# First attention of a two-block transformer kernel: its score products taken from high and low parts of queries and keys that are stacked over all 128 rows

## The reference, cut to what matters

```
def diff_attention_mixer(h, hc, w_in, lam, subln, w_out, lambda_init, ctx_out):
    ...
    q, k, v = project(h)
    qc, kc, vc = project(hc)
    q, k = apply_rope(q, cos, sin), apply_rope(k, cos, sin)
    ...
    def attend(qb, kb, vb):
        sc = jnp.einsum('blhid,bkhid->bihlk', qb, kb, preferred_element_type=jnp.float32) * scale
        p = jax.nn.softmax(sc, axis=-1)
        p = p[:, 0] - lam_full * p[:, 1]
        o = jnp.einsum('bhlk,bkhd->blhd', p.astype(vb.dtype), vb)
        o = rmsnorm(o, subln) * (1.0 - lambda_init)
        return o.reshape(o.shape[0], o.shape[1], DA_HEADS * DA_V_DIM)
```

## Time and profile before

| | |
|---|---|
| median of three runs | 2395.69 us (2393.03 to 2397.93) |
| profiled execution | 2393.02 us, its span 2391.1 us |
| TensorE busy | 2322.2 us, 97% of the span |
| granted TensorE clock, mean | 0.997 of full speed |
| VectorE, ScalarE, GpSimd busy | 1297.4, 971.0, 1340.2 us |
| the first attention's units | from 447.0 us (first score product) to about 650 us |

### The profile page before, as it was taken

One profiled execution on the slowest core, in us unless ns is written; L12 is line 12 of the kernel. 1 busy time (PEld: TensorE's weight loads), 2 busy tenths in 40 slices (PEclk: granted clock), 3 DMA queues, 4 the chain that ended last, 5 costly groups with the idle time before them and its releaser, 6 DMA issues.

```text
span 2391.1 us, 36091 instructions
## 1 busy us (share of the span) xinstructions
PE 2322.2 (97%) x14528; PEld 2068.9 (87%) x14528; DVE 1297.4 (54%) x2191; ACT 971.0 (41%) x1598; POOL 1340.2 (56%) x700
## 2 busy tenths in 40 slices
PE   7999999999989999999999998899999999999998
PEld 5888889777688888898888897799999999999998
DVE  8898296666578982966332035564324314534331
ACT  4322224455442332243223235454444444545443
POOL 3564465222135654654444442188879886468886
PEclk9999999999999999999999999999999999999999
DMA  6555362211025553625553331145555564345554
GB/s 271 211 192 178 110 219 85 71 62 54 27 80 212 194 176 110 220 93 187 192 178 108 98 93 62 45 168 185 176 166 179 180 195 150 98 148 187 182 178 135
DMA packets 97508, 350.09 MB, mean 146 GB/s; under 512 B 10944, under 2 KB 10944, under 8 KB 96960
## 3 DMA queue, kind: packets, MB, share of 16 engines
q1 hardware_dynamic: 97344, 347.81, 43.6%
HBM read 346.71 MB, written 1.05 MB: 145 GB/s over the span
## 4 chain that ended last, share of the span: by engine, by line
PE 62%; DVE 4%; ACT 2%; issue 1%; DMA 1%; POOL 1%; SPq 0%; DVEq 0%; ACTq 0%
PE psum L1573 20%; PE psum L1577 19%; PE psum L1574 19%; POOL w_lo L770 1%; PE psum L1922 1%; ACT w_hi L790 1%; PE psum L1894 1%; DMA w_raw<-in_ffn_out 0%; DVE psum L1131 0%; DVE psum L1211 0%; DVE h L1217 0%; PE psum L1902 0%; DVE u_lo L1431 0%; DVE pcomb L1404 0%; DVE stat L1489 0%
## 5 line engine op out<-in xcount | busy, mean ns | idle before, releaser
L770 POOL TENSOR_TENSOR w_lo<-w_raw,w_hi 128x1024 fp32r<-128x1024 f32 (+3 forms) x696 | 1340.0, 1946 | 1034.0 <-ACT w_hi L790 1033.2
L1573 PE MATMUL psum<-u_hi,w_hi 128*128 128x256 f32 (+2 forms) x2912 | 972.4, 334 | 10.9 <-POOL w_lo L770 7.7
L1577 PE MATMUL psum<-u_lo,w_hi 128*128 128x256 f32 (+2 forms) x2912 | 948.2, 326 | 3.5 <-DVE u_lo L1203 2.2
L1574 PE MATMUL psum<-u_hi,w_lo 128*128 128x256 f32 (+2 forms) x2912 | 946.5, 325 | 0.0
L790 ACT ACTIVATE w_hi<-w_raw 128x1024 fp32r<-128x1024 f32 (+1 forms) x522 | 537.4, 1032 | 438.8 <-PE psum L1577 343.2
L1573 PEld LDWEIGHTS psum<-u_hi,w_hi 128*128 128x128 f32 x2912 | 554.3, 190 | 78.8 <-issue 27.6
L1577 PEld LDWEIGHTS psum<-u_lo,w_hi 128*128 128x128 f32 x2912 | 553.6, 190 | 52.3 <-DVE u_lo L1203 5.3
L1574 PEld LDWEIGHTS psum<-u_hi,w_lo 128*128 128x128 f32 x2912 | 554.4, 190 | 45.5 <-issue 3.4
L1573 PE MATMUL psum<-gu_hi,w_hi 128*128 128x256 f32 (+1 forms) x1188 | 379.4, 319 | 0.2 <-POOL w_lo L770 0.2
L1574 PE MATMUL psum<-gu_hi,w_lo 128*128 128x256 f32 (+1 forms) x1188 | 378.1, 318 | 0.0
L1577 PE MATMUL psum<-gu_lo,w_hi 128*128 128x256 f32 (+1 forms) x1188 | 378.1, 318 | 0.0
(11 more groups left out here) (173 smaller groups left out, 1984.5 us busy)
## 6 DMA issues: line engine op xcount, KB each, us to landing
w_raw<-in_ffn_in SPq DMA_DIRECT2D x264, 512.0 KB, 3.5
w_raw<-in_ffn_out SPq DMA_DIRECT2D x96, 448.0 KB, 3.4
ada_hi<-in_ada_w SPq DMA_DIRECT2D x48, 512.0 KB, 5.2
ada_lo<-in_ada_w SPq DMA_DIRECT2D x48, 512.0 KB, 5.2
w_raw<-in_ffn_out SPq DMA_DIRECT2D x48, 512.0 KB, 3.6
ada_out<-in_ada_w SPq DMA_DIRECT2D x32, 512.0 KB, 3.8
w_raw<-in_b_qkv SPq DMA_DIRECT2D x30, 512.0 KB, 3.5
w_raw<-in_da_in SPq DMA_DIRECT2D x24, 512.0 KB, 3.5
```

The source lines that it names most:

```text
L770: last = pool.tensor_tensor(w_lo[:, slot, w], w_raw[:, slot, w], w_hi[:, slot, w].bitcast(F32), ALU.subtract)
L1573: mm(out, w_hi[:, slot, w], x_hi, start=start and n == 0, stop=False)
L1574: mm(out, w_lo[:, slot, w], x_hi, start=False, stop=False)
L1577: last = mm(out, w_hi[:, slot, w], x_lo, start=False, stop=stop and n == len(ks) - 1)
```

## The change

The scores of the first attention are made from high and low parts. For each head and each map m, `qa[:, room, m]` holds the high part of the map's query on its own 64 rows and the low part on the other 64. `ka[:, room, m]` holds the key's high part on both halves, `kb[:, room, m]` the key's low part on the map's own rows and zeros on the others. Two `float32r` products over 128 rows then give high by high plus low by high (L1994) and high by low (L1995). There are two rooms, for even and odd heads.

ScalarE makes the high copies, 64 x 512 each: two for a query, four for a key (a new list entry `split`). GpSimd makes the low parts, two subtractions of 64 x 512 for a query and two for a key, and once two memsets of `kb`. In the list the query's and key's `split` are put about one clock tick after their `rot`, and not before the scores of head s-2 are reached. On GpSimd a split comes after the low parts of all weight tiles up to the one behind the newest that the projections have begun (`behind`), and before all later tiles. TensorE waits for GpSimd (`split_part`) in place of the rotary result. The rotary temporaries, the raw q and k, v, probabilities and their like move to other places in SBUF; the raw key has one buffer, so ScalarE's evacuation of a key waits for GpSimd's split of the key before it.

```diff
@@ mixer_plan
+    def split(it):
+        nonlocal splits
+        splits += 1
+        it["split_n"], it["behind"] = splits, newest + 1
+        add("split", it)
+    def split_due():
+        while unsplit and unsplit[0][1] <= clock and scored >= 4 * unsplit[0][0]["s"] - 5:
+            split(unsplit.pop(0)[0])
...
+        if op == "rot" and kind == "da":
+            unsplit.append((it, clock + 1))
@@ GpSimd
+        def split_rest(x):
+            n = split_steps(x) - 2
+            pool.wait_ge(lo_ready, x["behind"] + 1)
+            pool.wait_ge(split_hi, x["split_n"])
+            if x["split_n"] == 1:
+                for m in range(2):
+                    pool.memset(kb[map_rows(1 - m), :, m, :].bitcast(F32), 0.0).then_inc(split_part, 1)
+                    pool.wait_ge(split_part, m + 1)
+            room, src = x["s"] % 2, item_stage(x)
+            for m in range(2):
+                own, across = map_rows(m), map_rows(1 - m)
+                if x["what"] == "q":
+                    pool.tensor_tensor(qa[across, room, m, :], src[own, :], qa[own, room, m, :].bitcast(F32),
+                                       ALU.subtract).then_inc(split_part, 1)
+                else:
+                    pool.tensor_tensor(kb[own, room, m, :], src[own, :], ka[own, room, m, :].bitcast(F32),
+                                       ALU.subtract).then_inc(split_part, 1)
+                pool.wait_ge(split_part, n + m + 1)
...
+        for x in (x for op, x, _ in plans["da"][0] if op == "split"):
+            rests(done, x["behind"] + 1)
+            done = x["behind"] + 1
+            split_rest(x)
+        rests(done, N_TILES)
@@ ScalarE
+                if kind == "da" and x["what"] != "v" and room_user(x):
+                    act.wait_ge(split_part, split_steps(room_user(x)))
...
+                elif op == "split":
+                    act.wait_ge(S["qk_ready"], x["rope_n"])
+                    if x["s"] >= 2:
+                        act.wait_ge(S["s_ready"], 4 * (x["s"] - 1))
+                    room, src = x["s"] % 2, item_stage(x)
+                    for m in range(2):
+                        own, across = map_rows(m), map_rows(1 - m)
+                        if x["what"] == "q":
+                            last = scalar.activation(qa[own, room, m, :], src[own, :], ACT.Copy)
+                        else:
+                            scalar.activation(ka[own, room, m, :], src[own, :], ACT.Copy)
+                            last = scalar.activation(ka[across, room, m, :], src[own, :], ACT.Copy)
+                    last.then_inc(split_hi, 1)
@@ TensorE
             def item_ready(it):
-                if it["rope"]:
+                if kind == "da":
+                    pe.wait_ge(split_part, split_steps(it))
+                elif it["rope"]:
                     pe.wait_ge(S["qk_ready"], it["rope_n"])
...
                     elif kind == "da":
+                        room, q0 = st["s"] % 2, x["qt"] * 128
                         for m in range(2):
-                            rows = slice(64 * m, 64 * m + 64)
-                            q0, k0 = place_of(st["q"][0]) + x["qt"] * 128, place_of(st["k"][0])
-                            last = mm(out[:, m, :], q_st[rows, q0:q0 + 128], k_st[rows, k0:k0 + n], start=True, stop=True)
+                            query = qa[:, room, m, q0:q0 + 128]
+                            mm(out[:, m, :], query, ka[:, room, m, 0:n], start=True, stop=False)
+                            last = mm(out[:, m, :], query, kb[:, room, m, 0:n], start=False, stop=True)
```

More of the change, by code:

```diff
@@ L258, in prepare_due @@
                 prepare(n)
-                return
+                break
+        split_due()
     def prepare_all(of):
@@ L265, in prepare_all @@
             if n is None:
+                while any(it is o for it, _ in unsplit for o in of):
+                    split(unsplit.pop(0)[0])
                 return
@@ L277, in mixer_plan @@
     add("first", first)
+    newest = max(it["t"] for it in first)
     clock += 16
@@ L638, in item_stage, with map_rows, room_user, split_steps @@
             off = it["g"] * SEQ
-            return vT[:, off:off + n]
+            return v_raw[it["kind"]][:, off:off + n]
+        if it["kind"] == "da":
+            return da_q[:, it["s"] % 2, :] if it["what"] == "q" else da_k[:, :]
         off = place_of(it)
         return (q_st if it["what"] == "q" else k_st)[:, off:off + n]
+    def map_rows(m):
+        return slice(64 * m, 64 * m + 64)
+    def room_user(it):
+        n = it["s"] - (2 if it["what"] == "q" else 1)
+        return next((x for op, x, _ in plans["da"][0] if op == "split" and x["what"] == it["what"] and x["s"] == n), None)
+    def split_steps(it):
+        return 2 * it["split_n"] + 2
     def latents(it):
+        if it["kind"] == "da":
+            return item_stage(it)[:, LAT]
         off = place_of(it) + width(it["tok"]) - SEQ
```

46 lines of the change are left out of this document (37 added, 9 removed).

## The result

The changed kernel takes 2408.22 us (median of 6 runs, 2403.93 to 2410.98), against 2394.66 us for the kernel before in the same series (6 runs). The ratio is 1.0056, 95% interval 1.0045 to 1.0066: slower by 13.6 us, where 4 us less had been forecast. The profiled execution's span is 2405.9 us, 14.8 above the 2391.1 of before. Of all executions of this document one, of the packed form, was in a slow state (3731.01 us at a granted clock of 0.573), and the ratios leave it out.

The account below looks back on a forecast made before the run. TensorE was taken to bound the attention's middle, other engines' work being free unless late. Terms -9.4 + 2.7 + 1.7 + 0.3 + 0.7 = -4.0 us gave 2389.0 profiled, 2391.7 us as median; range 2386 to 2398.

Parts of the forecast that it names:

- The units' gain, -9.4: Attention scores: shorter products save 8.9 us in units 0 to 26 and 0.5 in the last five.
- The start, +2.7: First unit: TensorE waits for head 0's split, so first scores start at 449.7 in place of 447.04.
- Rivals 1 and 2: Rival 1: start costs little, 2388.0, chance 0.24; rival 2: GpSimd's queue decides, 2400.3 at 2.4 us a subtraction, 0.10.
- The fall of the clock, +1.7: Behind the first unit's 4.2 us idle wait, TensorE runs four us at a granted clock of 0.57.
- The splits of the later heads, +0.3: Later heads: copies and subtractions stay covered, except that GpSimd's subtractions hold up VectorE, costing 0.3 us.
- The end, +0.7: Last units: head 7's key split delays the maximum of unit 27 and the last value evacuation, 0.7 us.
- Rival 3: New waits for split parts or at the units' end bring more clock falls, 1.7 us each; two give 2395.1; chance 0.13.

Follow-up runs that it names:

- the packed form: Changed kernel with weight tiles let ahead, unstacked: one copy and one subtraction per query and key, six 64-row products; 2397.81 us, ratio 1.0012 to the kernel before.
- the run with old products: Changed kernel with weight tiles let ahead and early clearing, but scores by float32 products over 64 rows from high copies alone; 2402.34 us, ratio 1.0036.
- the clock kept up: Changed kernel, old tile order, with 18 unused products on TensorE ahead of the first scores; 2408.32 us, ratio 1.0065 to the kernel before.
- the version with two rooms: Changed kernel with weight tiles let ahead, early clearing, unit 0's scores unsplit, head 0's key in its own buffer; 2395.37 us, ratio 1.0001.
- GpSimd's alone: Changed kernel with GpSimd's subtractions for heads 2 to 7 on 8 columns instead of 512; 2402.38 us, ratio 1.0033 to the kernel before.
- ScalarE's alone: Changed kernel with ScalarE's high copies for heads 2 to 7 on 8 columns instead of 512; 2406.98 us, ratio 1.0055 to the kernel before.
- both 10: Changed kernel, old tile order, with copies and subtractions of heads 2 to 7 on 8 columns; 2398.32 us, ratio 1.0017 to the kernel before.
- the run with both made small: The version with two rooms, with copies and subtractions of heads 2 to 7 on 8 columns; 2388.06 us, ratio 0.9967 to the kernel before.
- the version with tiles first: Changed kernel with two more weight tiles ahead of a split's subtractions on GpSimd from head 1 on; 2398.82 us, ratio 1.0020.

## Why the prediction was wrong

Step by step:

- **The units' gain, -9.4: right where TensorE has no wait.** 0.33 us at the unit shown; 7.5 us by the run with old products; 8.1 us from unit 4 to 27 (145.3 less 137.2) where 7.9 was reckoned. The first four units don't show it: with the clock kept up they take 24.5 us as before, where 1.4 less was reckoned, and what takes the 1.4 is not shown.
- **The start, +2.7: right.** +2.9 (449.9 less 447.0), by the same steps. That the sum fits so well is in part luck: GpSimd began 0.5 us later than reckoned (442.41, not 441.9), and its two clearings took 1.95 us and not 2.2. Rivals 1 and 2 fall with it: a subtraction takes 1.3 us, whether it crosses the halves of the rows (1298 ns in the mean) or not (1279).
- **The fall of the clock, +1.7: a little small.** 2.4 us by the difference between the run with the clock kept up and the changed kernel. By the Trainium skill (TensorE: Matmul & The Clock Gate, "The HAM clock gate") idleness brings the fall; the trace agrees at this place, 1.00 with the idle time filled and 0.77 without.
- **The splits of the later heads, +0.3: this step failed.** Units 4 to 27 take 153.9 us where 145.3 - 7.9 = 137.4 was forecast, so the term is 16.5 us there. Of them TensorE stands idle 10.7, and the lower clock takes 3.4 (the sum over stretches of 4 us of what is missing to full speed); the other 2.4 aren't traced. The prediction said of the weight tiles: "a split in between delays the tile behind it by 3 to 5 us, whose high part is made four tiles ahead. That stays covered." For TensorE it did stay covered, no tile came late in the middle. But a delayed tile comes together with the next one, GpSimd then works 7 us on end, and VectorE's instructions are held up once for each of GpSimd's. The prediction counted each hold as one subtraction's length beside 20 tiles "that are there today and are covered", as if the two would not meet.
- What the runs make of the 16.5: tiles ahead of the subtractions takes 10.1 (153.9 to 143.8; 6.5 of them idle time and 3.4 the clock), and copies and subtractions made small, on top of that, 6.3 (143.5 to 137.2, from the version with two rooms). ScalarE's copies and GpSimd's subtractions were not parted in that second step. With the tile order as it was, GpSimd's alone was worth 6 us of time, ScalarE's alone 1, both 10; the intervals of 5 to 8 us are too wide to say whether both together are more than the sum. Some of each is the clock: its 3.4 us in the middle are gone in the profiled executions of all of these. How much of that is the edits' is not shown, since with the clock kept up at the start it is 1.7 us by the same reckoning, with the same waits in the middle as in the changed kernel.
- **The end, +0.7: too small, as far as the profile shows.** Units 28 to 31 take 2.2 us more than before. No run parts what does it.
- **Rival 3** (more falls of the clock) was the nearest in kind: TensorE's wait at 519 to 522 was followed by a granted clock of 0.50 in 524 to 526, and a second wait, up to 583, by 0.57 in 584 to 588. But it was priced as two falls of 1.7 and without the waits that bring them. Nor does such a wait always bring one: with the clock kept up at the start, TensorE's wait of 2.58 us before 521.54 was followed by 1.00 in 522 to 526, where the changed kernel had 0.61 behind 2.55 us.

The sum with the measured terms: 2.9 + 2.4 - 7.9 + 16.5 + 2.2 - 1.3 = 14.8. It closes because the 16.5 is what is left over in the middle; the check on it is the run with both made small, where almost all of it is gone. The forecast used the smallest distance between exponentials and scores, 1.15 us, as a distance against ScalarE's copies. Against VectorE being held up by 1.2 and then 2.2 us more it was no cover.

## What to carry to other kernels

Work given to an idle engine is not free when a neighbour shares its way to the operands: reckon its longest stretch of work without a pause, not its busy share, and lay that stretch beside the neighbour's most urgent chain. When an instruction that waits for another engine is put into a list, everything behind it comes in a bunch afterwards; ask what the bunch does, and let ready work go first. And a shorter product pays only where the new preparation fits: here 8 us were there to be had (0.9967) and the copies, the subtractions and the start took nearly all of it even in the best order. Less preparation can be worth dearer products: the packed form is the one whole version in which TensorE has next to no wait from unit 4 to 27.

## What the runs showed of the hardware

- While GpSimd runs instructions of 2.35 us back to back, VectorE's instructions on SBUF get through one at a time: 128x1 in 1.34 us and 128x256 in 2.55 (0.16 and 0.34 in the version with tiles first, at 520.61 with GpSimd idle and at 516.70 with its tile about to end). The maximum, which reads PSUM, kept its time: 1.23 us at 463.73 in the version with two rooms, all of it beside a weight tile (463.16 to 465.61). The Trainium skill (SBUF — State Buffer, "SBUF: two separate sides") says that VectorE and GpSimd share a pair of ports, which a GpSimd instruction, or one of VectorE's in a two-port mode or with two inputs in SBUF, holds to its end while the other one waits. The trace agrees, and shows in addition that two GpSimd instructions on end hold up two VectorE instructions in turn.
- GpSimd's prices: subtraction of 64x512 1.28 to 1.30 us, clearing of 64x1024 0.95, subtraction of 64x8 0.20. It goes by columns: 128x512 took 1.50 to 1.54 in the packed form, so half the rows save a sixth at most.
- Six float32r products over 64 rows of 512 columns take 0.90 us (0.15 each) between two gaps of 0.10, four over 128 rows 0.92 without gaps: 1.56 against 1.39 us with their neighbours.
- Two of TensorE's waits of the same length at the same place, 2.55 and 2.58 us, were followed by a granted clock of 0.61 in one execution and of 1.00 in the other (522 to 526 us).
- VectorE's own subtraction of 64x512 takes 0.70 us undisturbed, and 0.82 and 1.12 in the mean beside the weight tiles.
